# Scores of the second block by pairs of query blocks, with second passes of 64 rows each

## The reference, cut to what matters

```python
for start in range(0, S, Q_BLOCK):                      # SB, 4 blocks of 128 queries
    qb, kb, vb = q[:, start:end], k[:, :end], v[:, :end]
    z = jnp.einsum('bqhd,bkhd->bhqk', qb, kb).astype(jnp.float32) * scale
    log_beta = jax.nn.log_sigmoid(z)
    log_1m_beta = jnp.where(strict, jax.nn.log_sigmoid(-z), 0.0)
    suffix = lax.cumsum(log_1m_beta, axis=3, reverse=True) - log_1m_beta
    w = jnp.where(strict, jnp.exp(log_beta + suffix), 0.0)
    outs.append(jnp.einsum('bhqk,bkhd->bqhd', w.astype(v.dtype), vb))
...
s = jnp.einsum('bnqhd,bnkhd->bnhqk', qc, k_band).astype(jnp.float32) * (d ** -0.5)   # CA
s = s + bias[None, None]
p = jax.nn.softmax(s, axis=-1)
```

## Time and profile before

| | |
|---|---|
| median of 3 runs | 956.82 us (956.42 to 957.24) |
| profiled execution | 956.64 us |
| its span in the trace | 954.9 us |
| granted TensorE clock | 1.00 of full in every stretch |
| attention of the second block | about 415 to 590 us from the span's start |

### The profile page before, as it was taken

The page is one execution under the profiler, slowest core; times in us unless marked ns, Lnnn a source line. Parts: engine busy times, 40 slices in busy tenths (PEclk is TensorE's granted clock), DMA queues, the critical chain, the costliest instruction groups (busy, mean ns, idle before and its releaser), DMA issues.

```text
span 954.9 us, 13280 instructions
## 1 busy us (share of the span) xinstructions
PE 943.2 (99%) x4728; PEld 788.2 (83%) x4728; DVE 689.8 (72%) x1270; ACT 562.5 (59%) x1107; POOL 93.1 (10%) x182
## 2 busy tenths in 40 slices
PE   8999999999999999999999999999999999999998
PEld 7878988888888887877788877898888888888887
DVE  6487888878788766677768886857544853673988
ACT  6448787753233247479987764556745634644562
POOL 5001111111122103000000000110000000000110
PEclk9999999999999999999999999999999999999999
DMA  8205222139787653833442423364877567486773
GB/s 302 89 24 190 68 78 90 50 151 350 278 331 264 207 133 126 304 121 95 129 175 68 131 67 129 139 174 133 206 213 176 167 195 191 120 231 193 171 187 110
DMA packets 34898, 156.57 MB, mean 164 GB/s; under 512 B 5241, under 2 KB 5497, under 8 KB 22162
## 3 DMA queue, kind: packets, MB, share of 16 engines
q1 hardware_dynamic: 21042, 103.51, 31.2%
q0 software_dynamic: 11152, 49.29, 20.9%
q10 hardware_dynamic: 2640, 2.93, 1.0%
HBM read 144.61 MB, written 5.27 MB: 157 GB/s over the span
## 4 chain that ended last, share of the span: by engine, by line
PE 86%; DVE 8%; ACT 2%; DMA 1%; issue 1%; ACTq 0%; POOL 0%; DVEq 0%; POOLq 0%
PE psum L2247 26%; PE psum L2249 25%; PE psum L2248 25%; PE psum L2416 3%; PE psum L2394 2%; PE psum L2445 2%; DMA raw<-in_wall 1%; PE psum L2440 1%; DVE wl L1306 1%; DVE p_sb L1506 1%; DVE ptl L1518 1%; PE psum L2678 1%; DVE hl L1345 1%; DVE xt L1341 1%; DVE acc L1358 0%
## 5 line engine op out<-in xcount | busy, mean ns | idle before, releaser
L2247 PE MATMUL psum<-hh,wh 128*128 128x512 f32 (+2 forms) x736 | 277.8, 377 | 0.7 <-DVE hl L1345 0.6
L2249 PE MATMUL psum<-hh,wl 128*128 128x512 f32 (+2 forms) x736 | 270.2, 367 | 0.0
L2248 PE MATMUL psum<-hl,wh 128*128 128x512 f32 (+2 forms) x736 | 270.1, 367 | 0.0
L1306 DVE TENSOR_TENSOR wl<-raw,wh 128x512 fp32r<-128x512 f32 x336 | 218.7, 685 | 38.7 <-ACT wh L726 38.1
L726 ACT ACTIVATE wh<-raw 128x512 fp32r<-128x512 f32 x336 | 193.3, 621 | 70.5 <-PE psum L2249 64.0
L2247 PEld LDWEIGHTS psum<-hh,wh 128*128 128x128 f32 x736 | 138.5, 188 | 24.4 <-DVE hl L1345 1.4
L2249 PEld LDWEIGHTS psum<-hh,wl 128*128 128x128 f32 x736 | 138.3, 188 | 23.0
L2248 PEld LDWEIGHTS psum<-hl,wh 128*128 128x128 f32 x736 | 138.7, 188 | 20.7 <-issue 1.2
L2247 PE MATMUL psum<-wh,ah 128*128 128x512 f32 x192 | 76.1, 396 | 0.4 <-ACT p_sb L872 0.4
L2249 PE MATMUL psum<-wh,al 128*128 128x512 f32 x192 | 74.9, 390 | 0.0
L2248 PE MATMUL psum<-wl,ah 128*128 128x512 f32 x192 | 74.8, 390 | 0.0
(11 more groups left out here) (367 smaller groups left out, 1729.5 us busy)
## 6 DMA issues: line engine op xcount, KB each, us to landing
raw<-in_wall SPq DMA_DIRECT2D x79, 1024.0 KB, 5.3
raw<-in_wall POOLq DMA_DIRECT2D x20, 1024.0 KB, 8.0
wa<-in_wada POOLq DMA_DIRECT2D x24, 512.0 KB, 6.0
gt<-in_wada POOLq DMA_DIRECT2D x20, 512.0 KB, 5.7
xt<-in_xcols SPq DMA_DIRECT2D x8, 264.0 KB, 7.9
cb<-c_rows SPq DMA_DIRECT2D x8, 264.0 KB, 3.3
x<-in_x SPq DMA_DIRECT2D x4, 512.0 KB, 10.3
x_kept<-x SPq DMA_DIRECT2D x4, 512.0 KB, 2.8
```

Of the source, the lines that this page charges most:

```text
L1306: e.tensor_tensor(lower_, raw_of(w, c), upper_.bitcast(F32), ALU.subtract).then_inc(v["wl"], 1)
L2247: e.matmul(out_, lh, rh, start=start, stop=False, skip_group_check=True)
L2248: e.matmul(out_, lh, rl, start=False, stop=False, skip_group_check=True)
L2249: return e.matmul(out_, ll, rh, start=False, stop=stop, skip_group_check=True)
```

## The change

`pieces_of` gets a flag, set for both groups of heads of the second block: two turns follow each other, then two scores. `score` does nothing for an odd query block; for an even one it issues the scores of blocks i+1 and i together. The two first passes are over 128 rows as before. The two second passes take 64 rows each: only the upper part of q by the lower part of k. Block i+1 uses the head's own rows, block i the other 64, so that they stand on different halves of the array's rows. For this the upper part of q has to lie on the other rows for the even blocks: `queries` on ScalarE writes it there with a second instruction over 2x128 columns, and `queries` on VectorE writes the lower part in two instructions, one for the odd blocks (other rows) and one for the even ones (own rows). The product of lower q by lower k, which the second pass used to hold, is no longer made. PACE_S, AGE and the DMAs are the same.

```diff
-def pieces_of(heads):
+def pieces_of(heads, paired=False):
...
                 out.append(("T", g, j))
-                if scores:
+                if paired:
+                    if j % 2 == 0:
+                        out += [scores.pop(0) for _ in range(min(2, len(scores)))]
+                elif scores:
                     out.append(scores.pop(0))
...
-            pieces_of(CA) + pieces_of(SB), PACE_S,
+            pieces_of(CA, True) + pieces_of(SB, True), PACE_S,
...
+        def blocks_of(x, b):
+            return x.rearrange("p (a b c) -> p a b c", a=2, b=2)[:, :, b, :]
...
                 for i in parts:
-                    e.activation(upper[i][64 * i:64 * i + 64, :], src[64 * i:64 * i + 64, :], ACT.Copy,
-                                 scale=scale).then_inc(a["qh"], 1)
+                    rows, other = slice(64 * i, 64 * i + 64), slice(64 - 64 * i, 128 - 64 * i)
+                    ins = e.activation(upper[i][rows, :], src[rows, :], ACT.Copy, scale=scale)
+                    if p >= 4:
+                        ins = e.activation(blocks_of(upper[i][other, :], 0), blocks_of(src[rows, :], 0), ACT.Copy,
+                                           scale=scale)
+                    ins.then_inc(a["qh"], 1)
...
+                    else:
+                        for b, place in ((1, other), (0, rows)):
+                            ins = e.scalar_tensor_tensor(blocks_of(both[i][place, :], b), blocks_of(src[rows, :], b),
+                                                         scale, blocks_of(both[i][rows, :], b).bitcast(F32),
+                                                         ALU.mult, ALU.subtract)
+                    ins.then_inc(v["ql"], 1)
...
-                if i == 3:
+                if h not in FG and i % 2:
+                    return
+                if i == (3 if h in FG else 2):
                     e.wait_ge(v["ql"], 2 * p + 1 + odd)
...
+                if h not in FG:
+                    for b in (i + 1, i):
+                        e.matmul(scores_at(h, b), q[:, 128 * b:128 * b + 128], k_up[:, 0:128 * b + 128], start=True,
+                                 stop=False, skip_group_check=True)
+                    for b in (i + 1, i):
+                        r = 64 * ((odd + b + 1) % 2)
+                        e.matmul(scores_at(h, b), q[r:r + 64, 128 * b:128 * b + 128], k_lo[r:r + 64, 0:128 * b + 128],
+                                 start=False, stop=True, skip_group_check=True).then_inc(t["score"], 1)
+                    return
```

More of the change, by code:

```diff
@@ L1451, in queries @@
                     e.wait_ge(a["qh"], 2 * p + i + 1)
-                    e.scalar_tensor_tensor(both[i][other, :], src[rows, :], scale, both[i][rows, :].bitcast(F32),
-                                           ALU.mult, ALU.subtract).then_inc(v["ql"], 1)
+                    if p < 4:
+                        ins = e.scalar_tensor_tensor(both[i][other, :], src[rows, :], scale,
+                                                     both[i][rows, :].bitcast(F32), ALU.mult, ALU.subtract)
+                    else:
[4 more added lines that the diff above has]
+                    ins.then_inc(v["ql"], 1)
             def keys(p, src, parts=(0, 1)):
```

## The result

The change makes the kernel slower. Its median is 967.43 us over four runs (967.4 to 969.52), against 957.0 us (956.42 to 957.24) for the kernel before: the ratio is 1.012, with a 95% interval of 1.0108 to 1.0132. The forecast was 954.7 with a range of 952.0 to 960.5, so both the sign and the range were wrong.

A forecast was written before the change was run, and what follows sets the result against it. TensorE, busy 943.2 of 954.9 us, was taken as the bound. ScalarE 1.3, second passes -1.9, order of turns -1.9 and VectorE 0.4 sum to -2.1, giving 954.7 us; range 952.0 to 960.5, by the terms' bounds 952.5 to 956.5.

The forecast's parts named there:

- Order of turns: Second block's attention: `ptl` moves ahead of VectorE's scans, so TensorE's three waits for it go, -1.9 us (0 to 1.9).
- its probabilities are turned nine beats after that: Score of 512 columns, issued two beats later: the turn of its probabilities comes nine beats after, with normalize at age six.
- Going between 128 and 64 rows: TensorE, 64 switches around second passes: taken as 0; other end 0.16 us each, 10.2 us, if the array empties.
- a start over 0.3 us after the first pass before: Profile sign on TensorE: if the first second pass starts that late, the array drains.
- Second passes: TensorE, paired scores: side by side saves 0.17 us a head (0.11 to 0.30); heads 13 to 23 count, -1.9 us.
- starts within 0.12 us: Profile sign on TensorE: a pair's two second-pass matmuls start this close; 0.23 apart would mean not side by side.
- ScalarE +1.3: Stretch 423 to 469: six extra q instructions, 2.1 us, less 0.8 usable free time, delay TensorE by 1.3 us at 469.
- VectorE +0.4: Lower q in two instructions, 0.136 us more, 16 times; 0.4 us exposed in the SB heads (0 to 1.1).
- Its other eight are hidden: From 515 ScalarE is busy 45.79 of 68 us, so its other eight extra q instructions there should cost nothing.
- ScalarE over 45.5 of 46 us busy: Profile sign, stretch 423 to 469: ScalarE this full, with TensorE's `qk` or `wl` wait up from 0.8 to some 2 to 3.
- Slower, by drains: Rival: each switch between 128 and 64 rows empties the array, 0.16 us each; +5.5, 962.3 us; chance 0.14.
- ScalarE and VectorE keep the gain: Rival: no free ScalarE time, `ptl` waits become score waits, VectorE's 1.1 shows whole; +1.3, 958.1 us; chance 0.18.

The follow-up runs named there:

- e7_turns_first: Kernel before with only the change's new order of pieces, single scores over 128 rows, q as before: 958.84 us, ratio 1.0026.
- e2_order_only: The change with second passes over 128 rows and q written as before, leaving new order and paired scores: 962.07 us, ratio 1.0055.
- e1_full_rows: The change with its second passes over 128 rows instead of 64; order, pairs and extra q instructions stay: 965.19 us, ratio 1.0092.
- e17_change_early_old_order: The change's 64-row second passes and new q writing, in the old order of pieces, pairs issued at the odd block's beat: 967.39 us, ratio 1.0117.
- e16_early_new_order: e2_order_only with each pair issued one beat earlier, at the odd block's beat: 959.52 us, ratio 1.0033.
- e8_pair_old_order: Kernel before, old order of pieces, with scores paired over 128 rows at the even block's beat, q as before: 975.13 us, ratio 1.0196.
- e15_early_old_order: Kernel before, old order of pieces, with scores paired over 128 rows at the odd block's beat, q as before: 959.78 us, ratio 1.0037.
- e4_one_half: The change with q as before and both 64-row second passes of a pair on the same half: 967.01 us, ratio 1.0112.
- e11_scalar_only: Kernel before with only ScalarE's extra q instruction, 16 of 64x2x128: 958.96 us, ratio 1.0024.
- e10_q_only: Kernel before with only the change's way of writing q, the extra instructions on ScalarE and VectorE: 960.69 us, ratio 1.0043.
- e12_vector_only: Kernel before with only VectorE's lower q split into two instructions, to the same rows: 957.29 us, ratio 1.0009.

## Why the prediction was wrong

The change's 10.4 us over before split by the chain of kernels that add one part at a time: new order of pieces with single scores +2.4 (e7_turns_first), pairs +3.0 (e2_order_only, 5.4 in all), q instructions +3.1 (e1_full_rows, 8.6), second passes on 64 rows +1.9 to 2.2 (the change). By the runs at a granted clock of 1.000 the last two are +2.0 and +2.9 to 3.3. This is one way through the parts; e17_change_early_old_order shows that on another way the shares are others. Against the terms of the prediction:

- **Order of turns, -1.9 (0 to -1.9): wrong in sign, +2.4 alone, +5.4 with the pairs.** This is the step that failed most. I read three waits for `ptl` in the earlier trace rows, saw that `ptl` moved ahead of a scan, and let the waits vanish. I wrote that the turn of block 0 comes a beat earlier, and did not ask that it meets the same bank sooner, nor what else stands ahead of `ptl` on VectorE: `qk`, which waits for ScalarE's root, and logits. In e7_turns_first this turn waits 0.88 us for it. And "its probabilities are turned nine beats after that" looked at the wrong reader of the later score: the sigmoid and the logits are to read it one beat behind its place in the list, which is the very beat at which the change issues the pair, and all that is queued behind them waits. In the change's order this lateness is worth 2.2 of the 3.0 us of the pairs (e16_early_new_order); where it is two beats it costs 15.2 (e8_pair_old_order against e15_early_old_order).
- **Going between 128 and 64 rows, taken as 0 (other end 0.16): the other end was right.** This is the second step that failed. e4_one_half against e2_order_only gives 0.155 each, 9.9 us for 64. The steps of 64-column tiles say nothing on 64 rows: that was the nearest row, and a different thing. The Trainium skill, page "TensorEngine Tiling (Array Packing)", section "Key Properties", says that changing the tiling mode drains TensorE. For rows the trace agrees: the load at 473.14 starts only 0.09 us after the matmul before it would have been through its columns. The prediction's own sign for it, a start over 0.3 us after the first pass before, was set too high: it is 0.26 in the change, behind a matmul of 384 columns that takes 0.18.
- **Second passes, saving 0.17 a head (0.11 to 0.30): right, a little low.** Side by side saves 0.24. The sign shown by the profile (starts within 0.12 us) came true. The Trainium skill, page "TensorE: Matmul & The Clock Gate", section "The mechanism", has tiles side by side start about 4 ns apart; the trace agrees with 3 ns, and even the loads run together. The other sentence of the Trainium skill there that the prediction quotes, that weight loads overlap with matmuls in flight only where the row group differs, is not what these traces show: at 128 rows the load at 472.42 starts with the matmul at 472.42.
- **ScalarE +1.3, VectorE +0.4: too small alone, near the mark in the sum.** Measured 2.4 and 0.8 alone, 4.3 together, and 2.0 to 3.1 behind the new order, whose waits hide a part. I had 0.35 for one instruction, it is 0.38 to 0.42, and the lateness isn't confined to the stretch before 469: e11_scalar_only has a turn that waits for `ptl` at 508.8 and one at 527.0 (0.54 and 0.48 us over a normal step) which before doesn't have. "Its other eight are hidden" failed. My sign for it, ScalarE over 45.5 of 46 us busy, did not appear in the change (41.78), since other waits made room. The sign that did appear, waits for `qk` and `wl` up from 0.8 to 3.1 us, is not the q instructions' doing: e2_order_only, without them, has 1.6 + 1.3.
- **The rivals.** "Slower, by drains" had the right mechanism and price, and 962.3. In the sum it was still 5 us short, as it kept the -1.9 of the turns. Of the 9.9 - 3.8 = 6.1 us that the rows cost TensorE net, some 3 show in the time, since TensorE's waits shrink by what it is late. "ScalarE and VectorE keep the gain" named the right engines, with 1.3 for what is 7.4 to 8.5 (order, pairs and q instructions). Neither case held both together, and the range was cut where the drains began. Its own range "by the bounds of the terms", 952.5 to 956.5, is not what those bounds add up to either: with the lower saving of nothing that the same text states, no gain at the turns and 2.1 and 1.1 for the two engines, the upper end is 3.2 over before, 960.0; the lower is 952.2.

What stays open: what the 3.5 us of e15_early_old_order over before consist of beyond its two new waits; why the first scores wait 0.6 us longer where VectorE's instruction is split (e10_q_only, e12_vector_only); and why the q instructions cost less behind the new order than alone. That VectorE's wait for ScalarE's second q instruction (it counts up only behind the second) is what passes the q cost on was not tried.

## What to carry to other kernels

When a move puts an instruction later in a list that several engines walk, ask first who reads its result at a fixed distance, and what is queued behind that reader; two beats cost 15.2 us in e8_pair_old_order. A term that has both signs of movement in it (a wait "goes", a turn comes earlier) should be read on the releasing engine: what stands in front of the releaser, and did that move? A stretch of 64 rows between matmuls of 128 pays about 0.155 us at each edge here, so two passes side by side have to save over 0.3 us to be worth it; the most that they saved is 0.17. And when several parts are added one after the other, the share of each depends on the order: the q instructions cost 4.3 us alone and 2.0 behind the new order.

## What the runs showed of the hardware that I had not expected

- Between 128-row and 64-row matmuls the next weights are not loaded ahead: the load starts with its matmul (473.14 and 473.56 in the change), 0.09 us after the matmul before it would have given way to one of its own height, and the first matmul of a new height takes 0.34 instead of 0.23 for 512 columns (473.56 to 473.90).
- In e4_one_half two 64-row matmuls of 512 and 384 columns on the same half start 0.34 apart, and their loads 0.11. This is the same thing: the first of them is the first of a new height, just as the product at 473.56 in the change, whose next load starts 0.11 behind it (473.67).
- On different halves two loads of 64 rows start 3 to 4 ns apart in the change and take 0.19 us together; their matmuls start 3 ns apart as well.
- From 128 to 64 *columns* of weights there is no such price, 0.12 from start to start for 256 columns.
